# Second expert stage of a two-block decoder kernel: experts 2 to 15 in an order made on chip, and pairs of 96 and 64 slots in place of 96 and 96

## The chip, the cores and the metric

The kernel runs on one core of a Trainium2 chip. Its time is the device time of one launch in microseconds (us). All data are 32-bit floats.

## What is computed

Two decoder blocks run one after the other over 512 tokens of width 1024. Each has a token mixer (not touched here) and a mixture of experts. The second block's mixture has 16 experts in 4 groups; each token goes to two experts of its best group, so 1024 pairs of a token and an expert are to be computed:

```python
N_EXPERTS_2 = 16;  TOP_K = 2;  EXPERT_HIDDEN = 512;  D_MODEL = 1024
def hier_moe_2(x, w_group, b_group, w_expert, b_expert, w_gate, w_up, w_down):
    t = x.reshape(-1, D)
    pg = jax.nn.softmax((t @ w_group + b_group).astype(jnp.float32), axis=-1)
    ...
    gates = jnp.sum(jax.nn.one_hot(expert_id, N_EXPERTS_2, dtype=jnp.float32) * weights[..., None], axis=1)
    for e in range(N_EXPERTS_2):
        h = jax.nn.silu(t @ w_gate[e]) * (t @ w_up[e])
        y = y + gates[:, e:e + 1] * (h @ w_down[e])
```

For the inputs of this case the reference sends 69, 62, 64, 63, 63, 73, 58, 44, 88, 72, 73, 77, 39, 56, 55 and 68 tokens to experts 0 to 15.

## The kernel before

The first block's expert stage (32 experts, weights of 1 MB a matrix) is the "narrow" one and stays as it is. The second block's is the "wide" one (`z.wide`): 8 bodies of two experts, experts 2i and 2i+1 in body i. Each expert has a gate, an up and a down matrix of 2 MB. There is one buffer for each expert of a pair: `z.expert(0)`, called `ring` in the trace, and `z.expert(1)`, called `arena_moe`. A load for the next body can therefore only be issued when TensorE has used the matrix that lies there.

Each expert has 96 slots (`cap`), a body 192: expert A's 96 and expert B's first 32 fill the 128 partitions of units 0 and 1, and expert B's other 64 are unit 2. TensorE works in tiles of 32 rows of output: four such tiles, each with its own 32 tokens and its own part of a weight matrix, run side by side. In a body it makes

- unit 0 of gate and up (`gate_up`, L2385): 8 steps of four products of 512 columns;
- unit 1 and unit 2 (`gates_before_ups`, L2396): each first 8 steps of gates, then 8 of ups, of four products of 256 columns. Unit 2 has the 64 slots of expert B twice, once for each half of the hidden width;
- the turning of the hidden values (`turn_hidden`, L2440) between these;
- the turning of the token rows of the next body (`turn_rows_pe`, L1953), in two halves; for body 1 a gather by products with a one-hot matrix stands in its place (`gather_pe`, L1937);
- `down_first` (L2453): two products of 8 steps for units 0 and 1, and `down_second` (L2465): 4 steps of four products of 512 columns for unit 2.

TensorE's counts that others wait for are `gates`, `hidden` (units done), `down` (down products done). SyncE's queue issues the weights in a fixed order, each after such a count: gate and up of expert A, gate and up of expert B (L1577), down of A, down of B (L1583). GpSimd fetches the token rows of body i+2 from `normed_rows` by an indirect transfer (`fetch_rows`, L1911) and places the results in `expert_rows` (`place_rows`, L1918 and L1921). ScalarE makes the silu and moves the results out of the banks, VectorE multiplies gate by up (L2511) and scales the turned rows (`turned_rows_dve`, L1962).

Which token sits in which slot comes from a table in memory, `slot_table`, with a row for every rank and expert. VectorE counts (`out_programs.rounds`), computes ranks, positions and weights (`entries`), GpSimd writes the table (L1848), SyncE reads it back (`load_slots`, L1591). If an expert has more than 96 tokens, further rounds over all bodies are run from `Further.run`; the largest count decides. In the trace no such round runs.

The last body's rows aren't placed in memory: `all_sums_pe` (L1996) adds them to the residual through products with a one-hot matrix, while eight loads of 512 KB (`load_outputs`, L2039) bring back what the other bodies placed. They are issued when unit 1 of the last body is done. VectorE adds them (`add_outputs_dve`, L2048), makes the low parts of the last body's results (`y_low_dve`, L2025), and adds the sums (`add_sums_dve`, L2055).

Of the kernel before, what the change touches and what calls it, by code (L numbers as in the profile page):

```python
# [15 lines left out]
P = 128  # L16
S = 512
# [1468 lines left out]
class Moe:  # L1486


    def __init__(self, m, d, experts, per_group, slots, block):
# [7 lines left out]
        self.loads = 64 if self.wide else 32  # L1497
        self.most = -(-S // slots)
# [14 lines left out]
        at = self.extra.end  # L1513
        self.now_fetch, at = m.view(at, 2, dt=I32)
# [24 lines left out]
        for i in range(9):  # L1539
            self.one[i], s = m.view(s, NT)  # L1540
        self.ring23, end = m.view(m.arena_size - 2 * RING, 2, RING)
# [24 lines left out]

    def weights_of(self, io, name, e):

        w = io[name][0]
        return w[e] if isinstance(e, int) else w[bass.ds(e, 1)].rearrange("e a b -> (e a) b")  # L1570

    def load_in(self, sp, io, s, body, sem, parts=(0, 1)):

        both, _ = self.expert(s) if self.wide else self.slot(s)
        for k in parts:
            w = self.weights_of(io, self.weights[k], body * self.EB + s)
            sp.dma_start(both[:, k], w.rearrange("(p c) n -> p c n", p=P)).then_inc(sem, 16)  # L1577

    def load_down(self, sp, io, s, body, sem):

        _, down = self.expert(s) if self.wide else self.slot(s)
        w = self.weights_of(io, self.weights[2], body * self.EB + s)
        sp.dma_start(down, w.rearrange("(c p) n -> p c n", p=P)).then_inc(sem, 16)  # L1583

    def load_slots(self, engine, slots, first_rank, sem):
# [7 lines left out]
        if self.wide:  # L1593
            part(0, 0, 0, 0, self.cap)
# [3 lines left out]
        else:  # L1598
            part(0, 0, 0, 0, 64)
            part(64, 0, 1, 0, 64)  # L1600

# [10 lines left out]
def out_programs(m, io, z, ph, residual, residual_scale, w_out_sem, gain, router, ring_sems):  # L1612
# [116 lines left out]
    def vector(dve):  # L1729
# [35 lines left out]
        v.mark(dve.tensor_scalar(z.upper, m.tokens[:, 0:1], float(64 - S), None, ALU.is_ge))  # L1765
        for k in range(2):
# [44 lines left out]
    def entries(dve):  # L1811

        split(dve, NT - 1)
        v = Chain(dve, ph.sem("weights"))
        for k in range(2):
# [15 lines left out]
    def rounds(dve):  # L1831

        v = Chain(dve, ph.sem("counting"))
        dve.wait_ge(ph.sem("totals"), 1)
        v.link(dve.tensor_reduce(z.stat[:, 0, 0:1], m.banks[7][:, 0:E], AX_X, ALU.max))
# [22 lines left out]

def front_products(pe, m, k, chunks):
# [6 lines left out]
class Further:  # L1866
# [5 lines left out]
    def run(self, engine, begin, body, end):  # L1872
# [4 lines left out]
        with engine.If(n > 0):  # L1877
            with engine.Fori(0, n) as r:
                begin(r)
                with engine.Fori(0, z.bodies) as i:  # L1880
                    body(r * z.bodies + i, i)
# [8 lines left out]
def slots_known(engine, z, slots, known, done):  # L1890
# [10 lines left out]
    if z.wide:  # L1901
# [3 lines left out]
    engine.wait_ge(known, done + KNOWN)  # L1905


def fetch_rows(pool, ph, z, fetch):

    for c, count in enumerate((P, z.slots - P)):  # L1910
# [4 lines left out]
def place_rows(pool, ph, z, place, c):  # L1915

    if z.wide and c == 1:
# [8 lines left out]
def gather_pe(pe, ph, z, pair, half, taken, last_split=None):  # L1926

    for a in range(2):
        if taken is not None:
            pe.wait_ge(ph.sem("gathered_taken"), taken + a + 1)  # L1930
        for b in range(2):
            j = 4 * half + 2 * a + b
            for t in range(NT):
                if last_split is not None and j == 0 and t == NT - 1:
                    pe.wait_ge(last_split, NT)
                for part in (z.x_hi, z.x_lo):
                    last = pe.matmul(pair[a][:, b * z.slots:(b + 1) * z.slots], part[:, t, j * P:(j + 1) * P], z.G[:, t, :],  # L1937
# [4 lines left out]
def turn_rows_pe(pe, ph, m, z, pair, half, arrived, taken):  # L1942
# [3 lines left out]
    for a in range(2):  # L1946
        if taken is not None:
            pe.wait_ge(ph.sem("gathered_taken"), taken + a + 1)
        for b in range(2):
            j = 4 * half + 2 * a + b  # L1950
            for c, count in enumerate((P, z.slots - P)):
                at = b * z.slots + c * P
# [4 lines left out]
def turned_rows_dve(dve, ph, m, z, pair, gain, n, half):  # L1957

    for a in range(2):
        dve.wait_ge(ph.sem("gathered"), 4 * n + 2 * half + a + 1)  # L1960
        j = 4 * half + 2 * a
        dve.tensor_tensor(z.xe[:, j:j + 2, :], pair[a][:, 0:2 * z.slots].rearrange("p (j n) -> p j n", j=2),  # L1962
                          m.params[:, gain + j:gain + j + 2].unsqueeze(2).broadcast_to([P, 2, z.slots]),
# [6 lines left out]
def onehot_dve(dve, ph, m, z, body):  # L1970

    cap, e = z.cap, body * z.EB
    if z.wide:
        own = cap - 64
        qa, qb, count = z.q[:, :, e:e + 1], z.q[:, :, e + 1:e + 2], m.slots[:, 1:2, :]
        dve.tensor_tensor(z.G[:, :, 0:cap], count[:, :, 0:cap].broadcast_to([P, NT, cap]), qa.broadcast_to([P, NT, cap]), ALU.is_equal)
        dve.tensor_tensor(z.G[:, :, cap:P], count[:, :, 64:cap].broadcast_to([P, NT, own]),
                          qb.broadcast_to([P, NT, own]), ALU.is_equal).then_inc(ph.sem("onehot"), 1)
        dve.tensor_tensor(z.G[:, :, P:P + 64], count[:, :, 0:64].broadcast_to([P, NT, 64]),
                          qb.broadcast_to([P, NT, 64]), ALU.is_equal).then_inc(ph.sem("onehot"), 1)  # L1980
# [6 lines left out]

def sums_pe(pe, ph, m, z, t, c, last_part):
# [1553 lines left out]
```

## Time and profile before

| what | value |
|---|---|
| median of 3 runs | 1460.3 us (1455.28 to 1463.12) |
| span of the profiled execution | 1458.0 us |
| granted TensorE clock, mean | 0.972 |
| PE busy | 1346.8 us, 92% |
| DVE / ACT / POOL busy | 500.6 / 369.4 / 313.7 us |
| moved by the DMA engines | 284.08 MB, mean 195 GB/s |

The profiled execution's own time is one of those in the first line; what lies around its span isn't given apart, so the span stands 2.3 us under the median. A busy share is a mean over stages with different limits; the second expert stage with its router is the part from about 1130 us on, its eight bodies lie between 1147 and 1439 us.

### The profile page before, as it was taken

The page shows a single profiled execution, that of the slowest core. Times are in us where ns is not written, and L with a number is a line of the kernel's source. Part 1 is how long each engine was busy: PE and PEld are TensorE (multiplying, and loading weights), DVE is VectorE, ACT ScalarE, POOL GpSimd, SP SyncE. Part 2 cuts the span into 40 slices and gives each one's busy share as a digit, 9 for nine tenths or more (in the row PEclk, how much of TensorE's full clock was granted, in tenths as well). Part 3 has the DMA queues.
Part 4 walks back from the last instruction along what each step waited for, and adds up shares of the span by engine and source line. Part 5 has one row for each costly group of instructions (what it writes and reads, how often), then busy time and mean ns, then how long its engine had stood idle before and what let it go on. Part 6 is the DMA issues. An engine that isn't in the chain of part 4 may idle for free. (4 is left out here: it accounts for less than half of the span.)

```text
span 1458.0 us, 27226 instructions
## 1 busy us (share of the span) xinstructions
PE 1346.8 (92%) x11948; PEld 869.5 (60%) x11948; DVE 500.6 (34%) x906; ACT 369.4 (25%) x682; POOL 313.7 (22%) x357
## 2 busy tenths in 40 slices
PE   6999989888899999998969999998899899999995
PEld 4878764577745554454448878895545654444442
DVE  4367425442233321111283167654523201000016
ACT  2223026444133011111142241324423011111112
POOL 8436202255000200000023523440000301111100
PEclk9999999999999999999979999999999899999998
DMA  5911100300062799999941121103062589999983
GB/s 160 342 68 58 58 1 0 117 4 5 4 249 101 280 416 417 415 418 417 411 170 59 58 79 37 59 2 116 1 248 103 209 325 376 387 378 387 381 330 148
DMA packets 75596, 284.08 MB, mean 195 GB/s; under 512 B 15217, under 2 KB 16568, under 8 KB 63186
## 3 DMA queue, kind: packets, MB, share of 16 engines
q1 hardware_dynamic: 68464, 267.47, 47.4%
q0 software_dynamic: 5440, 10.58, 2.1%
q10 hardware_dynamic: 1570, 4.24, 0.7%
q8 instruction: 97, 1.59, 0.5%
q14 instruction: 25, 0.20, 0.0%
HBM read 259.41 MB, written 29.84 MB: 198 GB/s over the span
## 5 line engine op out<-in xcount | busy, mean ns | idle before, releaser
L2396 PE MATMUL banks<-arena_moe,mixT 128*32 128x256 f32 x1280 | 113.5, 379 | 0.0
L391 POOL TENSOR_TENSOR arena_mix<-ring 128x512 f32<-128x512 f32 (+1 forms) x56 | 72.8, 1317 | 173.4 <-PE banks L426 128.3
L436 ACT ACTIVATE arena_mix<-banks 128x256 f32<-128x256 f32 x108 | 41.1, 383 | 258.4 <-PE banks L426 258.4
L1921 POOL DMA_INDIRECT expert_rows<-arena_moe x21 | 20.5, 978 | 388.5 <-ACT arena_moe L2220 161.3
L1648 PE MATMUL banks<-ring,mixT 128*128 128x512 f32 x224 | 99.1, 595 | 3.9 <-PEq L50 3.1
L426 PE MATMUL banks<-ring 128*128 128x256 f32 x432 | 100.1, 380 | 2.7 <-DVE arena_mix L447 1.6
L426 PEld LDWEIGHTS banks<-ring 128*128 128x128 f32 x432 | 81.2, 190 | 16.5 <-issue 5.8
L1962 DVE TENSOR_TENSOR mixT<-banks,params 128x512 f32<-128x512 f32 (+1 forms) x64 | 39.9, 625 | 143.3 <-PE banks L1937 85.3
L447 DVE SCALAR_TENSOR_TENSOR arena_mix<-banks,arena_mix 128x256 f32<-128x256 f32 x81 | 33.1, 422 | 160.2 <-ACT arena_mix L436 90.0
L1937 PE MATMUL banks<-G_moe,x_hi_moe 128*128 128x256 f32 (+1 forms) x320 | 81.3, 294 | 2.9 <-issue 2.9
L426 PE MATMUL banks<-ring,arena_mix 128*128 128x256 f32 x336 | 78.7, 389 | 2.8 <-POOL arena_mix L391 1.9
L1937 PE MATMUL banks<-G_moe,x_lo_moe 128*128 128x256 f32 (+1 forms) x320 | 79.6, 288 | 0.0
L426 PE MATMUL banks<-mixT,ring 128*128 128x256 f32 x336 | 76.8, 383 | 1.3 <-DVE mixT L318 1.3
L426 PEld LDWEIGHTS banks<-ring,arena_mix 128*128 128x128 f32 x336 | 64.8, 195 | 15.9 <-issue 7.2
L2396 PEld LDWEIGHTS banks<-arena_moe,mixT 128*32 128x32 f32 x1280 | 60.3, 109 | 22.0 <-issue 1.3
L1648 PEld LDWEIGHTS banks<-ring,mixT 128*128 128x128 f32 x224 | 41.5, 190 | 52.4 <-issue 52.4
L2511 DVE TENSOR_TENSOR mixT<-mixT,banks 128x256 f32<-128x256 f32 x24 | 10.1, 421 | 177.0 <-ACT mixT L2543 177.0
L426 PEld LDWEIGHTS banks<-mixT,ring 128*128 128x128 f32 x336 | 64.1, 192 | 10.9 <-DVE mixT L318 1.5
L1937 PEld LDWEIGHTS banks<-G_moe,x_hi_moe 128*128 128x128 f32 x320 | 63.9, 200 | 6.0 <-issue 6.0
L2120 PE MATMUL banks<-arena_moe,mixT 128*64 128x512 f32 x256 | 59.9, 621 | 7.1 <-DMA arena_moe<-in_exp_w_up 7.1
L1937 PEld LDWEIGHTS banks<-G_moe,x_lo_moe 128*128 128x128 f32 x320 | 64.0, 200 | 0.0
L2453 PE MATMUL banks<-ring,mixT 128*32 128x512 f32 x384 | 56.5, 594 | 1.9 <-issue 1.9
(453 smaller groups left out, 2564.1 us busy)
## 6 DMA issues: line engine op xcount, KB each, us to landing
ring<-in_w_in SPq DMA_DIRECT2D x26, 1024.0 KB, 7.7
arena_moe<-in_exp_w_gate SPq DMA_DIRECT2D x16, 1024.0 KB, 12.4
arena_moe<-in_exp_w_up SPq DMA_DIRECT2D x16, 1024.0 KB, 16.4
arena_moe<-in_exp_w_down SPq DMA_DIRECT2D x16, 1024.0 KB, 16.0
ring<-in_exp_w_gate SPq DMA_DIRECT2D x16, 1024.0 KB, 11.7
ring<-in_exp_w_up SPq DMA_DIRECT2D x16, 1024.0 KB, 14.3
ring<-in_exp_w_down SPq DMA_DIRECT2D x16, 1024.0 KB, 17.7
arena_moe<-in_w_gate SPq DMA_DIRECT2D x8, 2048.0 KB, 11.7
```

The source lines that it names most:

```text
L391: pool.tensor_tensor(out[:, c], a[:, c], b[:, c], op).then_inc(ph.sem("weight_sums"), 1)
L426: last = pe.matmul(self.m.banks[bank][:, 0:256], left, right, start=(k == 0 and j in (1, 2, 7)), stop=(k == 3), skip_group_check=True)
L436: act.activation(self.dest(n, i)[block], self.m.banks[a][:, 0:256], ACT.Copy, scale=self.scale(n)).then_inc(ph.sem(name), 1)
L447: dve.scalar_tensor_tensor(out, self.m.banks[c if j == 2 else d][:, 0:256], self.scale(n), out, ALU.mult, ALU.add).then_inc(ph.sem(name), 1)
L1648: last = pe.matmul(m.banks[k % 3][:], m.mixT[:, c, i * P:(i + 1) * P], w[:, c, :], start=(c == 0), stop=(c == DC - 1), skip_group_check=True)
L1921: pool.indirect_dma_start(z.d.outputs, bass.IndirectOffsetOnAxis(ap=place[:, c:c + 1].bitcast(U32), axis=0), z.y[:, 2 * c:2 * c + 2, :].re ...
L1937: last = pe.matmul(pair[a][:, b * z.slots:(b + 1) * z.slots], part[:, t, j * P:(j + 1) * P], z.G[:, t, :], start=(t == 0 and part is z.x_h ...
L1962: dve.tensor_tensor(z.xe[:, j:j + 2, :], pair[a][:, 0:2 * z.slots].rearrange("p (j n) -> p j n", j=2), m.params[:, gain + j:gain + j + 2]. ...
L2120: last = pe.matmul(hb[u][k * cap:(k + 1) * cap, :], z.xe[:, j, s * cap:(s + 1) * cap], both[:, :, j, :], start=(j == 0), stop=(j == DC - 1))
L2396: last = pe.matmul(hb[u][T * k:T * (k + 1), 256 * part:256 * part + 256], z.xe[:, j, at:at + T], both[:, part, j, half * 256:half * 256 + ...
L2453: last = pe.matmul(yb[n][T * i:T * (i + 1), :], z.hT[:, h, f, T * i:T * (i + 1)], wd[:, 2 * half + f, n * HW:(n + 1) * HW], start=(h == 0 ...
L2511: dve.tensor_tensor(z.hid[:, u, :], z.hid[:, u, :], hb[u][:, 256:512], ALU.mult).then_inc(ph.sem("hidden_done"), 1)
```

## The change

Bodies 1 to 7 no longer hold experts 2i and 2i+1. VectorE ranks experts 2 to 15 by their counts on chip; the seven with the most tokens take the even positions 2, 4, ..., 14, the other seven the odd ones 3, 5, ..., 15, in order. So body 1 has the largest and the eighth, body 7 the seventh and the last. Body 0 keeps experts 0 and 1 and 96 and 96 slots. A pair of bodies 1 to 7 has 96 and 64 slots: 160. A further round now also runs if more than 7 of experts 2 to 15 have over 64 tokens.

The packing into tiles of 32 is new. Unit 0 (`packed_gate_up`) needs only expert A, unit 1 (`packed_gates_before_ups`) has the rest of A and two tiles of B, and the third unit (`packed_rest`) is B's last 32 slots: its four tiles are gate and up, each in two halves, of 256 columns, half a unit. `packed_down_second` has products of 256 columns. Its results are quarters of a row, which `place_rows` writes as quarters, and which `quarter_sums_pe` sums in the last body.

```diff
@@ order_experts, new; called at the start of entries()
+    v.link(dve.scalar_tensor_tensor(z.keys, z.totals, float(E), z.tie, ALU.mult, ALU.add))
+    v.link(dve.tensor_tensor(z.pairs[:, 2:, 1:], z.keys[:, 1:].unsqueeze(1).broadcast_to([P, E - 2, E - 1]),
+                             z.keys[:, 2:].unsqueeze(2).broadcast_to([P, E - 2, E - 1]), ALU.is_gt))
+    v.link(dve.tensor_reduce(z.greater[:, 2:], z.pairs[:, 2:, 1:], AX_X, ALU.add))
...
+    return dve.tensor_copy(z.expert_at, z.greater)
@@ sync of wide_programs
-        z.load_slots(sp, z.main, 0, ph.sem("slots"))
+        load_main_slots(sp, z, ph.sem("slots"))
+        sp.wait_ge(out.sem("ordered"), 1)
         for i in range(1, NB):
-            for s in range(2):
-                sp.wait_ge(ph.sem("gates"), 2 * i + s - 1)
-                z.load_in(sp, io, s, i, ring[s], (0,))
-                sp.wait_ge(ph.sem("hidden"), 3 * i + s - 1)
-                z.load_in(sp, io, s, i, ring[s], (1,))
+            e = [chosen(2 * i + s) for s in range(2)]
+            sp.wait_ge(ph.sem("gates"), 1 if i == 1 else i + 1)
+            z.load_in(sp, io, 0, i, ring[0], (0,), e[0])
+            sp.wait_ge(ph.sem("hidden"), 3 * i - 1)
+            z.load_in(sp, io, 0, i, ring[0], (1,), e[0])
+            if i == 1:
+                sp.wait_ge(ph.sem("gates"), 2)
+            else:
+                sp.wait_ge(ph.sem("hidden"), 3 * i)
+            z.load_in(sp, io, 1, i, ring[1], (0,), e[1])
+            sp.wait_ge(ph.sem("hidden"), 3 * i)
+            z.load_in(sp, io, 1, i, ring[1], (1,), e[1])
@@ tensor of wide_programs, the third unit and the second down product of bodies 1 to 7
+        def packed_rest(i):
+
+            both, _ = z.expert(1)
+            for j in range(DC):
+                for k in range(4):
+                    part, half = k // 2, k % 2
+                    last = pe.matmul(hb[2][T * k:T * (k + 1), 0:256], z.xe[:, j, P:P + T],
+                                     both[:, part, j, half * 256:half * 256 + 256], start=(j == 0), stop=(j == DC - 1),
+                                     skip_group_check=True)
+            last.then_inc(ph.sem("hidden"), 1)
...
+            for h in range(2):
+                for f in range(2):
+                    for k in range(4):
+                        last = pe.matmul(yb[2][T * k:T * (k + 1), 0:256], z.hT[:, 2, f, T * h:T * h + T],
+                                         wd[:, 2 * h + f, 256 * k:256 * k + 256], start=(h == 0 and f == 0),
+                                         stop=(h == 1 and f == 1), skip_group_check=True)
@@ quarter_sums_pe, new
+    for flip in range(2):
+        if flip == 1:
+            pe.wait_ge(ph.sem("quartered"), 2 * t + 4)
+        for part in (z.y_hi, z.y_lo):
+            for k in range(2):
+                g = (k + flip) % 2
+                for n in range(2):
+                    a = 64 * n + 32 * g
+                    last = pe.matmul(m.banks[2 * (t + k) + n][:, 256 * g:256 * g + 256], z.ST[a:a + 32, 1, (t + k) * P:(t + k + 1) * P],
+                                     part[a:a + 32, 2, 0:256], start=False, stop=(part is z.y_lo), skip_group_check=True)
```

Where the instructions stand. On TensorE, in the last body, the pieces around the third unit and the second down product. Before:

```order
L2396 MATMUL banks<-ring,mixT 32x256 x3
L2396 MATMUL banks<-arena_moe,mixT 32x256
L2440 MATMUL banks<-ident,mixT 128x128 x2
L2396 MATMUL banks<-arena_moe,mixT 32x256 x64
L2440 MATMUL banks<-ident,mixT 128x128 x2
L2453 MATMUL banks<-ring,mixT 32x512 x3
L2453 MATMUL banks<-arena_moe,mixT 32x512
L2440 MATMUL banks<-ident,mixT 128x128 x2
L2465 MATMUL banks<-arena_moe,mixT 32x512 x16
L1996 MATMUL banks<-x_hi_moe,G_moe 128x512 x32
```

After:

```order
L2580 MATMUL banks<-ring,mixT 32x256 x2
L2580 MATMUL banks<-arena_moe,mixT 32x256 x2
L2670 MATMUL banks<-ident,mixT 128x128 x2
L2591 MATMUL banks<-arena_moe,mixT 32x256 x32
L2670 MATMUL banks<-ident,mixT 128x128 x2
L2614 MATMUL banks<-ring,mixT 32x512 x3
L2614 MATMUL banks<-arena_moe,mixT 32x512
L2600 MATMUL banks<-ident,mixT 128x64 x2
L2626 MATMUL banks<-arena_moe,mixT 32x256 x16
L2135 MATMUL banks<-x_hi_moe,G_moe 128x512 x8
L2122 MATMUL banks<-x_hi_moe,G_moe 128x256 x16
L2135 MATMUL banks<-x_hi_moe,G_moe 128x512 x8
```

The third unit has 32 products for 64, the second down product 16 of 256 columns for 16 of 512; nothing moved past anything else, and the trace counts each of these products as two records.

On VectorE, between the one-hot matrix of body 0 and the ranks. Before:

```order
L1979 TENSOR_TENSOR G_moe<-slots,arena_moe 128x4x64
L1727 TENSOR_TENSOR x_lo_moe<-arena_moe,x_hi_moe 128x1024
L1816 TENSOR_TENSOR arena_moe<-arena_moe 128x64 x2
L1819 TENSOR_REDUCE arena_moe<-arena_moe 128x4 x2
L1821 TENSOR_REDUCE arena_moe<-arena_moe 128x4
```

After:

```order
L1764 TENSOR_TENSOR x_lo_moe<-arena_moe,x_hi_moe 128x1024
L1940 SCALAR_TENSOR_TENSOR arena_moe<-arena_moe 128x16
L1941 TENSOR_TENSOR arena_moe<-arena_moe 128x14x15
L1943 TENSOR_REDUCE arena_moe<-arena_moe 128x14
L1944 TENSOR_SCALAR arena_moe<-arena_moe 128x14
L1945 SCALAR_TENSOR_TENSOR arena_moe<-arena_moe 128x14
L1946 TENSOR_SCALAR arena_moe<-arena_moe 128x16
L1948 TENSOR_TENSOR arena_moe<-arena_moe,experts 128x256
L1949 TENSOR_TENSOR arena_moe<-arena_moe,experts 128x256
L1950 TENSOR_REDUCE arena_moe<-arena_moe 128x16
L1951 CAST arena_moe<-arena_moe 128x16
L1857 TENSOR_TENSOR arena_moe<-arena_moe 128x64 x2
```

Ten operations of the ordering stand ahead of the ranks, ten more for ranks by position follow them, and the counting of rounds before this piece has nine operations for four.

On SyncE's queue, between the down loads of one body and the gate load of the next. After (before, L1583 for expert B is followed by L1577 at once):

```order
L1601 DMA ring<-in_w_down 128x4x1024
L1601 DMA arena_moe<-in_w_down 128x4x1024
L2486 TENSOR_LOAD arena_moe
L2486 ISA x2
L2486 TENSOR_LOAD arena_moe
L2486 ISA x2
L1595 ISA
L1595 DMA ring<-in_w_gate 128x4096
L1595 DMA ring<-in_w_up 128x4096
```

Two reads of an expert's number into registers stand ahead of each body's loads (an ISA row is a wait or a register step).

## Rows read from the trace of the kernel before

**Rows 1.** The page, part 2: 40 slices of 36.45 us, GB/s moved.

```profile
GB/s 160 342 68 58 58 1 0 117 4 5 4 249 101 280 416 417 415 418 417 411 170 59 58 79 37 59 2 116 1 248 103 209 325 376 387 378 387 381 330 148
```

**Rows 2.** Chain that ended last, 1170 to 1439 us: start, duration, what.

```profile
1170.48 3.56 PE banks L1937 x32
...
1188.54 6.87 PE banks L2385 x64
...
1260.34 6.87 PE banks L2385 x64
...
1274.49 7.04 PE banks L2396 x128
...
1283.60 7.01 PE banks L2453 x64
...
1292.67 3.57 PE banks L2465 x32
1296.24 6.87 PE banks L2385 x64
...
1425.50 1.88 issue
1427.38 7.07 PE banks L2453 x64
...
1438.93 2.73 PE banks L1996 x12
```

**Rows 3.** Timeline of SyncE's queue: start, duration, line, transfer issued.

```profile
1198.92 0.34 SPq L1577 DMA_DIRECT2D ring<-in_w_gate  x1
...
1260.45 0.38 SPq L1583 DMA_DIRECT2D arena_moe<-in_w_down  x1
1270.72 0.34 SPq L1577 DMA_DIRECT2D ring<-in_w_gate  x1
...
1417.77 0.34 SPq L2039 DMA_DIRECT2D ring<-expert_rows  x1
```

**Rows 4.** Windows 1200 to 1202 us: engines, granted clock, DMA share, GB/s.

```profile
1200.00:1201.00 1.00, 1.00 (x24) 0.65 (x20) 0.00 (x0) 0.00 (x0) 0.00 (x0) 1.00 0.46 98
1201.00:1202.00 1.00, 1.00 (x27) 0.54 (x16) 0.00 (x0) 0.00 (x0) 0.00 (x0) 1.00 1.05 426
```

**Rows 5.** DMA view of one body, 1260.34 to 1296.24 us.

```profile
DMA packets 2038, 13.66 MB, mean 381 GB/s; under 512 B 248, under 2 KB 248, under 8 KB 1523
...
q1 hardware_dynamic: 1587, 12.40, 88.5%
q0 software_dynamic: 448, 1.21, 10.8%
...
arena_moe<-in_w_down SPq DMA_DIRECT2D x1, 2048.0 KB, 13.8
```

**Rows 6.** DMA view, 500 to 700 us, the first expert stage.

```profile
DMA packets 15960, 83.38 MB, mean 417 GB/s; under 512 B 2336, under 2 KB 2336, under 8 KB 9254
```

**Rows 7.** Windows of 2 us within the same body.

```profile
1266.34:1268.34 2.00, 2.00 (x37) 0.97 (x31) 0.42 (x1) 0.38 (x1) 0.00 (x0) 1.00 1.03 293
...
1284.34:1286.34 2.00, 2.00 (x24) 0.65 (x20) 0.00 (x0) 0.00 (x0) 0.00 (x0) 1.00 1.04 442
```

**Rows 8.** VectorE's timeline, 1129 to 1150 us.

```profile
1129.25 0.23 DVE L1792 TENSOR_TENSOR arena_moe<-arena_moe 128x64 f32<-128x64 f32 x1
...
1141.31 0.56 DVE L1962 TENSOR_TENSOR mixT<-banks,params 128x384 f32<-128x384 f32 x1 [4.04 <-PE banks L1937]
...
1149.62 1.02 DVE L1962 TENSOR_TENSOR mixT<-banks,params 128x384 f32<-128x384 f32 x2 [5.17 <-remote]
```

**Rows 9.** Timeline, 1433 to 1442 us, the end of the stage.

```profile
1433.07 1.23 DVE L2048 TENSOR_TENSOR arena_moe<-arena_moe 128x1024 f32<-128x1024 f32 x1
...
1434.21 0.75 DVE L2025 SCALAR_TENSOR_TENSOR x_hi_moe<-banks,arena_moe,x_hi_moe 128x512 fp32r<-128x512 f32 x1
...
1441.78 2.35 DVE L2055 TENSOR_TENSOR arena_moe<-arena_moe,banks 128x1024 f32<-128x1024 f32 x2 [1.31 <-PE banks L1996]
```

More of the change, by code:

```diff
@@ L1540, in __init__ @@
             self.one[i], s = m.view(s, NT)
+        if self.wide:
+            self.totals, s = m.view(s, experts)
+            self.keys, s = m.view(s, experts)
+            self.pairs, s = m.view(s, experts, experts)
+            self.greater, s = m.view(s, experts)
+            self.later, s = m.view(s, experts)
         self.ring23, end = m.view(m.arena_size - 2 * RING, 2, RING)
@@ L1593, in load_slots @@
         if self.wide:
-            part(0, 0, 0, 0, self.cap)
+            part(0, 0, 0, 32, self.cap)
             part(self.cap, 0, 1, 64, self.cap - 64)
@@ L1814, in entries @@
         v = Chain(dve, ph.sem("weights"))
+        if z.wide:
+            order_experts(dve, v, m, z).then_inc(ph.sem("ordered"), 1)
+            for k in range(2):
+                v.mark(dve.tensor_tensor(t[4 + k], t[k], z.later.unsqueeze(1).broadcast_to([P, NT, E]), ALU.mult))
+            v.wait()
+            for k in range(2):
+                v.mark(dve.tensor_reduce(one[7 + k], t[4 + k], AX_X, ALU.add))
+            second_ranks(dve, v, z, t[4], t[5])
         for k in range(2):
@@ L1870, in __init__, with run @@
         self.m, self.z, self.known = m, z, known
-    def run(self, engine, begin, body, end):
+    def run(self, engine, begin, body, end, written_out=False):
         z = self.z
@@ L1879, in run @@
                 begin(r)
-                with engine.Fori(0, z.bodies) as i:
-                    body(r * z.bodies + i, i)
+                if written_out:
+                    for i in range(z.bodies):
+                        body(r * z.bodies + i, i)
+                else:
+                    with engine.Fori(0, z.bodies) as i:
+                        body(r * z.bodies + i, i)
             end(n)
@@ L2399, in gates_before_ups, with packed_gate_up @@
                 last.then_inc(ph.sem("gates" if part == 0 else "hidden"), 1)
+        def packed_gate_up(i):
+            pe.wait_ge(ring[0], 32 * i + 32)
+            for j in range(DC):
+                if j % 2 == 0:
+                    pe.wait_ge(ph.sem("gathered_taken"), 4 * i + j // 2 + 1)
+                for k, (s, at, half) in enumerate(packed[0]):
+                    both, _ = z.expert(s)
+                    last = pe.matmul(hb[0][T * k:T * (k + 1), :], z.xe[:, j, at:at + T], both[:, :, j, half * 256:half * 256 + 256],
+                                     start=(j == 0), stop=(j == DC - 1), skip_group_check=True)
+            last.then_inc(ph.sem("hidden"), 1)
@@ new lines, in packed_gates_before_ups @@
+        def packed_gates_before_ups(i):
+            pe.wait_ge(ring[1], 32 * i + 32)
+            for part in range(2):
+                for j in range(DC):
+                    for k, (s, at, half) in enumerate(packed[1]):
+                        both, _ = z.expert(s)
+                        last = pe.matmul(hb[1][T * k:T * (k + 1), 256 * part:256 * part + 256], z.xe[:, j, at:at + T],
+                                         both[:, part, j, half * 256:half * 256 + 256], start=(j == 0), stop=(j == DC - 1),
+                                         skip_group_check=True)
+                last.then_inc(ph.sem("gates" if part == 0 else "hidden"), 1)
@@ new lines, in packed_rest @@
+        def packed_rest(i):
+            both, _ = z.expert(1)
+            for j in range(DC):
+                for k in range(4):
+                    part, half = k // 2, k % 2
+                    last = pe.matmul(hb[2][T * k:T * (k + 1), 0:256], z.xe[:, j, P:P + T],
+                                     both[:, part, j, half * 256:half * 256 + 256], start=(j == 0), stop=(j == DC - 1),
+                                     skip_group_check=True)
+            last.then_inc(ph.sem("hidden"), 1)
```

302 lines of the change are left out of this document (228 added, 74 removed).

## Prediction

> **What bounds the kernel now.** The change lies in the second expert stage, the last 310 us. I read the page's slices first: there the transfers run at 376 to 387 GB/s through the stage, against 415 to 418 in the first expert stage [rows 1]. So both the weights' transfers and TensorE could be the limit, and the next view must say which. The chain of work that ended last is TensorE alone: each body repeats the same pieces, body 3 begins at 1260.34 and body 4 at 1296.24, 35.90 us apart, with no wait in between [rows 2]; the other bodies repeat this to 0.1 us. TensorE is the limit.
>
> The reader must then ask how far behind the transfers are. SyncE issues expert B's down load at 1260.45; it lands 13.8 us later, at 1274.3, while the next body's first gate load was issued at 1270.72 [rows 3, 5]. The queue has not emptied when the next load enters. In that one body the 16 DMA engines moved 13.66 MB and were taken 88.5% by the weights' queue and 10.8% by the token rows' queue [rows 5]: 99.3% of 35.9 us. The transfers are a second limit just under the first.
>
> **The change, part by part.**
>
> TensorE. A packed body (1 to 7) has a third gate-and-up unit of half the columns, and a second down product of half the columns. The unit of 256-column products takes 7.04 us, the down product 3.57 [rows 2]; half of each is 3.52 and 1.79. That a 256-column product costs half of a 512-column one can be seen in the same rows: 64 of 512 columns take 6.87 us, 128 of 256 take 7.04. The transposes of the rows keep their number; I give them nothing. So a body falls from 35.90 to 30.6 us. For seven bodies (the last too) TensorE alone would save 37 us. The token rows of body 1 are gathered in 160 columns for 192: from nothing to 1.2 us (a sixth of its two pieces of 3.56 [rows 2]); I take nothing.
>
> Transfers. Nothing is taken away from them. The same sixteen experts are loaded, in another order, and only real tokens' rows are fetched and placed, about 128 a body as before. So a body still needs the 13.66 MB. What time does it need for them when TensorE no longer sets the pace? From below: the first expert stage sustained 417 GB/s over 200 us [rows 6], which gives 32.8 us. From above: the 35.9 us that it has now, of which the engines are taken 99.3%. Inside a body the rate is 442 GB/s while gates and ups are loaded, and 293 while down loads and token rows run side by side [rows 7]. The own mix is the nearer row, which speaks for the upper end. But in a queue that is never short of work the token rows will fall beside other loads, and the gaps between loads close, as in the first stage. I choose 34.2 us, near the middle. This is above 30.6: **the transfers become the limit.**
>
> The chain of the transfers. Body 1 starts at 1188.54 and its first 10.3 us are as before, so gate load 2 is issued at 1198.92 [rows 3] and the queue, which had been idling, fills at 1201.0 [rows 4]. From there it always has work: in a packed body the two down loads enter at 26.8 and 30.6 us, the next gate load 10.3 later. Each body adds 34.2 us. The down weights of body 7 are there at 1201.0 + 6 x 34.2, less 2 us since the last of these bodies fetches no rows (half of its token traffic, 10.8% of 35.9) = 1404.2. TensorE alone would be at body 7's first down product at 1188.54 + 6 x 30.6 + 18.0 (14.15 for two units and a turn, 3.52, 0.37 for a turn) + 1.9 (the stall before it, the 1.88 marked issue) = 1392.0. The later one counts: 1404.2 in place of 1427.38 [rows 2], a gain of 23.2 us. Bodies 1 and 2 run at 30.6; the first wait for down weights is in body 3 or 4.
>
> The end. After the last down weights SyncE's queue holds eight loads of placed rows, 4.19 MB, now issued at 1417.77 [rows 3], in time. They will stand behind the down loads: at 381 GB/s 11.0 us, until 1415.2. VectorE then adds the last two parts (2 x 1.23) and only behind them makes two low parts (2 x 0.75) [rows 9]: 1419.2, and the final sums begin. TensorE is ready at 1404.2 + 9.7 (11.5 from 1427.38 to 1438.93, less 1.79) = 1413.9. So the sums begin 15.0 us after the down product, and not 11.5: 3.5 us given back. The sums themselves are split in quarters, in two rounds with a wait of TensorE on its own results: not shown by any row; from nothing (four products side by side) to 1.5 us (half the time from 1438.93 to the first add at 1441.78 [rows 2, 9]); I take 0.6.
>
> The front. VectorE gets some 25 more small operations ahead of the entries of the slot table, each step about 0.23 us [rows 8]: 5.9 us. Behind them stand the first multiplication of the gathered rows, which TensorE waits for, and the slot table. VectorE had idled 4.0 us before that multiplication and 5.2 before the third [rows 8], so most is covered: nothing to 5.9 us, I take 1.5. The table comes 6 us later, but its rows are wanted only at the end of body 1. The register loads of the expert numbers stand on SyncE between the last down load and the next gate load, where it waits 10.3 us (1260.45 to 1270.72, [rows 3]): nothing, as long as two of them take less.
>
> Sum: 23.2 - 3.5 - 0.6 - 1.5 = 17.6 us, so 1458.0 becomes 1440.4. The median of the three runs stands 2.3 above the profiled span; with it **1443 us**.
>
> **The rivals.**
>
> A, forecast: the queue of the transfers takes over, at 32.8 to 35.5 us a body. Chance 0.75.
>
> B, the queue has no room: the slow mix of down loads and token rows is a matter of the chip and stays, 35.9 us a body. For it: 99% taken now. Against: 417 GB/s over 200 us [rows 6]. Body 7's down weights come at 1414.4, the gain is 13.0 - 5.6 = 7.4 us: 1453. Chance 0.13. The Trainium skill goes further this way: its page "SBUF — State Buffer", section "Summary: rules for kernel authors", says to reckon with about 358 GB/s between HBM and SBUF, by which a body's 13.66 MB would need 38 us and no cut on TensorE could help. By that rule the trace disagrees (381 GB/s over this body), and the skill's "HBM Reference", section "Specifications (TRN2)", has about 425 for a core that streams alone, which the 417 and 442 bear out.
>
> C, TensorE stays the limit: it needs the queue to do a body in under 31 us, 440 GB/s with the token rows in it; only windows without such rows show that [rows 7]. Gain 35.4 - 2.1: 1427. Chance 0.04.
>
> D, the other side: the loads now take their address from a register, and no load of the stage before did. If the queue can't prepare such a load while another runs, each pays the start again: the queue stood nearly 2.1 us from issue to full rate (1198.92 to 1201.0, [rows 3, 4]). Six a body are 12.6 us, 46.8 us a body; after six of them 75.6 us more than the forecast, 1518 us. It decides from 0.5 us a load (17.6 / 36 loads). Nothing in the rows speaks for it. Chance 0.05. (Were over 7 of experts 2 to 15 above 64 tokens, a whole further round would come; for these inputs 6 are.)
>
> The rest, 0.03, is a front or an end that costs more than a few us.
>
> **The numbers.** With 32.8 us a body the gain is 26.0 (1434), with 35.9 it is 7.4 (1453); the front may cost 4.4 more or 1.5 less. Range 1432 to 1454. Half a per cent (7.3 us) is what a measurement can tell. Slower: D and a little, 0.06. Same: over half of B and of the rest, 0.09. Faster: 0.85.
>
> **What would show it.** The chain of the stage, now TensorE alone, has waits for the down weights in bodies 3 or 4 to 7, some 3.5 us each, and starts of bodies 34.2 us apart where the first ones lie 30.6 apart. GB/s rises to 400 over a body. The third unit shows 64 products in 3.5 us. The final sums wait for VectorE's low parts. It would be wrong if bodies stay 30.6 apart to the end (C), if they lie above 35.5 apart (B or D), or if body 0 starts more than 4 us later.

## The result, and the profile after

| | kernel before | changed kernel |
|---|---|---|
| median, 4 runs each | 1461.7 us (1455.3 to 1467.4) | **1440.7 us** (1439.4 to 1443.1) |
| ratio to before | | 0.987, 95% interval 0.984 to 0.990 |
| span of the profiled execution | 1458.0 us | 1438.9 us |
| PE busy | 1346.8 us, 92% | 1313.6 us, 91% |
| DVE busy | 500.6 us | 506.9 us |
| moved by the DMA engines | 284.08 MB | 284.03 MB |

The change takes 21 us off, 15 to 23 by the interval. 1443 was forecast, 1432 to 1454 as range.

The page's slices of the changed kernel, GB/s moved in each 36 us, beside [rows 1]:

```profile
GB/s 162 344 71 59 59 1 0 118 4 5 4 233 93 275 414 418 415 417 416 415 243 33 86 59 59 59 1 102 17 139 142 206 307 350 409 411 412 394 392 150
```

The slices of the stage, 376 to 387 before, are 409 to 412 now. The chain that ended last, beside [rows 2] (start, duration, what):

```profile
1186.83 6.87 PE banks L2569 x64
1193.70 6.91 PE banks L2580 x128
...
1200.98 3.59 PE banks L2591 x64
...
1215.53 1.86 PE banks L2626 x32
1217.39 6.87 PE banks L2569 x64
1224.26 6.91 PE banks L2580 x127
...
1235.75 20.47 DMA arena_moe<-in_w_up
1256.26 7.11 PE banks L2580 x128
...
1267.96 22.25 DMA arena_moe<-in_w_up
1290.26 8.80 PE banks L2580 x127
...
1303.65 19.65 DMA arena_moe<-in_w_up
1323.34 7.12 PE banks L2580 x128
...
1335.04 24.24 DMA arena_moe<-in_w_up
1359.33 8.81 PE banks L2580 x128
...
1384.93 6.87 PE banks L2569 x64
1391.80 7.16 PE banks L2580 x122
```

Body 1 takes 30.56 us (1186.83 to 1217.39), with the third unit at 3.59 and the second down product at 1.86. Then each of bodies 3 to 6 has one wait in the chain, always at the same place: unit 1 (L2580) waits for expert B's up matrix. That load is issued right behind the third unit of the body before, which frees its buffer, and lands 20 to 24 us later, where a load needs 5 us of the engines alone (2.1 MB at 412 GB/s): it stands behind others in the queue. Unit 1 takes 7.1 us behind some waits and 8.8 behind others: in those the granted clock was at the lower level for a part of the unit (0.50 from 1292 to 1294, where it is 1.00 through the unit at 1323.34).

The chain doesn't show every wait. These four come to 9.1 us (1.44, 3.22, 0.62 and 3.78), and TensorE waits once more, for the down weights of body 5, on a stretch that the chain does not go through:

```profile
1337.73 0.63 PE L2614 MATMUL banks<-ring,mixT 128*32 128x512 f32 x3 [1.36 <-DMA arena_moe<-in_w_down]
```

The DMA view of 100 us in the middle of the stage (1260 to 1360), before and then after:

```profile
DMA packets 5815, 38.17 MB, mean 382 GB/s; under 512 B 808, under 2 KB 808, under 8 KB 4378
```

```profile
DMA packets 6137, 41.22 MB, mean 412 GB/s; under 512 B 708, under 2 KB 708, under 8 KB 4592
```

The share of packets under 512 B is near the same (14% and 12%) and the rate is 8% higher. The timelines of TensorE and VectorE at the end (the bracket is the idle time ahead and who ended it), beside [rows 9]:

```profile
1405.11 0.63 PE L2614 MATMUL banks<-ring,mixT 128*32 128x512 f32 x3 [1.87 <-issue]
...
1412.82 1.93 PE L2626 MATMUL banks<-arena_moe,mixT 128*32 128x256 f32 x32 [0.37 <-ACT mixT L2805]
1417.60 3.55 PE L2135 MATMUL banks<-x_hi_moe,G_moe 128*128 128x512 f32 x8 [2.84 <-DVE x_hi_moe L2170]
1421.08 0.57 PE L2122 MATMUL banks<-x_hi_moe,G_moe 32*128 32x256 f32 x8
1421.80 0.51 PE L2122 MATMUL banks<-x_hi_moe,G_moe 32*128 32x256 f32 x8 [0.15 <-PE banks L2122]
```

```profile
1405.22 1.22 DVE L2193 TENSOR_TENSOR arena_moe<-arena_moe,ring 128x1024 f32<-128x1024 f32 x1 [5.41 <-DMA arena_moe<-expert_rows]
...
1416.04 1.80 DVE L2170 SCALAR_TENSOR_TENSOR x_hi_moe<-banks,arena_moe,x_hi_moe 128x512 fp32r<-128x512 f32 x3
1422.62 2.35 DVE L2200 TENSOR_TENSOR arena_moe<-arena_moe,banks 128x1024 f32<-128x1024 f32 x2 [4.78 <-PEq L2127]
```

TensorE waits 2.84 us for VectorE's low parts, which stand behind eight early additions; the sums then run at the lower clock (0.53 granted; 3.55 us for eight products, where the next eight of that size take 2.08 in the same timeline).

**Where the 19.1 us between the two spans come from.** Part of it lies ahead of the stage, in code that the change doesn't touch: the last group of products of the routing (L1672, now L1709) starts at 1123.46 before and at 1119.94 after, 3.5 us. From there to body 1: 65.08 before, 66.89 after, 1.8 lost. From body 1 to the last body's first down product: 238.84 and 218.28, 20.6 gained. From there to the first of the last additions (L2055, now L2200): 14.40 and 17.51, 3.1 lost. The rest is equal. 3.5 - 1.8 + 20.6 - 3.1 = 19.2.

### The profile page after: what moved, and what is told of

The parts are those of the page before. It is cut to its first block and busy times, and to the rows that moved or that the text cites. A ratio compares the mean times of both kernels' runs of the same rounds, so it can differ in the third digit from the quotient of the medians.

```text
span 1438.9 us, 26499 instructions
## 1 busy us (share of the span) xinstructions
PE 1313.6 (91%) x11516; PEld 854.5 (59%) x11516; DVE 506.9 (35%) x938; ACT 367.1 (26%) x682; POOL 313.6 (22%) x358
## 2 busy tenths in 40 slices
DMA packets 75339, 284.03 MB, mean 197 GB/s; under 512 B 14966, under 2 KB 16317, under 8 KB 62930
## 5 line engine op out<-in xcount | busy, mean ns | idle before, releaser
L2081 DVE TENSOR_TENSOR mixT<-banks,params 128x512 f32<-128x512 f32 (+2 forms) x64 | 38.1, 596 | 139.3 <-PE banks L2056 80.5
L2056 PE MATMUL banks<-G_moe,x_hi_moe 128*128 128x256 f32 (+2 forms) x320 | 82.2, 296 | 2.8 <-issue 2.8
L2056 PE MATMUL banks<-G_moe,x_lo_moe 128*128 128x256 f32 (+2 forms) x320 | 80.5, 291 | 0.0
L426 PEld LDWEIGHTS banks<-ring,arena_mix 128*128 128x128 f32 x336 | 64.1, 192 | 13.3 <-issue 4.9
L2580 PE MATMUL banks<-ring,mixT 128*32 128x256 f32 x448 | 53.0, 398 | 9.1 <-DMA arena_moe<-in_w_up 9.1
L2757 DVE TENSOR_TENSOR mixT<-mixT,banks 128x256 f32<-128x256 f32 x17 | 7.2, 421 | 139.9 <-ACT mixT L2797 139.9
L2265 PE MATMUL banks<-ring,mixT 128*64 128x512 f32 x256 | 56.3, 592 | 0.0
L2321 DVE TENSOR_TENSOR mixT<-mixT,banks 128x256 f32<-128x256 f32 x16 | 6.7, 422 | 131.9 <-ACT mixT L2355 131.9
## 6 DMA issues: line engine op xcount, KB each, us to landing
ring<-in_exp_w_gate SPq DMA_DIRECT2D x16, 1024.0 KB, 12.8
ring<-in_exp_w_down SPq DMA_DIRECT2D x16, 1024.0 KB, 17.6
```

Source lines behind the costliest of these rows:

```text
L426: last = pe.matmul(self.m.banks[bank][:, 0:256], left, right, start=(k == 0 and j in (1, 2, 7)), stop=(k == 3), skip_group_check=True)
L2056: last = pe.matmul(pair[a][:, b * width:(b + 1) * width], part[:, t, j * P:(j + 1) * P], z.G[:, t, 0:width], start=(t == 0 and part is z.x ...
L2081: dve.tensor_tensor(z.xe[:, j:j + 2, 0:width], pair[a][:, 0:2 * width].rearrange("p (j n) -> p j n", j=2), m.params[:, gain + j:gain + j + ...
L2265: last = pe.matmul(hb[u][k * cap:(k + 1) * cap, :], z.xe[:, j, s * cap:(s + 1) * cap], both[:, :, j, :], start=(j == 0), stop=(j == DC - 1))
L2580: last = pe.matmul(hb[1][T * k:T * (k + 1), 256 * part:256 * part + 256], z.xe[:, j, at:at + T], both[:, part, j, half * 256:half * 256 + ...
```

## The experiments

Since what lies ahead of the stage moves from profile to profile, the runs are read within it. The columns, worked out from the chain or timeline of each profiled execution: start of the last group of routing products; from there to body 1; from unit 1 of body 1 to unit 1 of body 7 (six bodies); from there to the first of the last additions. Then the time: the median of four to eight executions, of two for the changed kernel with half down, and of a single one for three quarters, fewer rows, fixed addresses, longer front and both fillings of the wait.

| run | routing | to body 1 | six bodies | end | time, us |
|---|---|---|---|---|---|
| kernel before | 1123.5 | 65.1 | 215.4 | 31.0 | 1461.7 |
| changed kernel | 1119.9 | 66.9 | 198.1 | 30.8 | 1440.7 |
| before, half down | 1123.1 | 64.4 | 215.4 | 31.0 | 1462.0 |
| after, half down | 1122.6 | 65.8 | 183.4 | 30.0 | 1428.7 |
| after, three quarters | 1130.2 | 64.0 | 185.6 | 30.1 | 1434.7 |
| after, fewer rows | 1124.0 | 63.0 | 195.5 | 29.4 | 1437.4 |
| after, fixed addresses | 1119.3 | 66.5 | 197.4 | 30.2 | 1438.3 |
| before, longer front | 1124.0 | 66.8 | 215.4 | 31.0 | 1462.0 |
| after, four products in the wait | 1126.0 | 62.5 | 198.5 | 28.6 | 1440.3 |
| after, two products in the wait | 1125.8 | 67.4 | 198.6 | 28.5 | 1445.0 |
| after, two rows to a partition | 1122.7 | 67.0 | 197.8 | 29.7 | 1443.2 |
| after, low parts first | 1128.2 | 63.8 | 198.3 | 28.1 | 1438.3 |
| after, finer order | 1118.4 | 66.6 | 198.0 | 28.6 | 1442.6 |
| after, both edits | 1131.0 | 66.8 | 197.4 | 27.3 | 1442.8 |

### Is it the transfers? Half of the down weights, in both kernels

```diff
@@ load_down
-        sp.dma_start(down, w.rearrange("(c p) n -> p c n", p=P)).then_inc(sem, 16)
+        kept = 2 if self.wide and body > 0 else down.shape[1]
+        sp.dma_start(down[:, 0:kept], w.rearrange("(c p) n -> p c n", p=P)[:, 0:kept]).then_inc(sem, 16)
```

> The changed kernel with only half of each down matrix loaded for bodies 1 to 7 (the results of those experts are wrong for that half; every product is still made). Theory, the transfers limit the changed stage: a body needs 11.6 MB for 13.7, about 28 us of the queue, less than TensorE's 30.6. The waits for weights in bodies 3 to 6 go, all bodies start 30.6 us apart, body 7's first down product comes 203 us after body 1's start and not 218, and the final sums no longer wait for VectorE's low parts: 1440.7 becomes about 1423. Rival, the bodies' 33 to 35 us come from something else than the amount moved (addresses from registers, the slower clock, the order in which buffers come free): under 4 us faster, bodies still 33 us and more apart.

> The kernel before with the same halving of its down loads (wrong results for that half). Theory, TensorE alone limits the stage before: bodies stay 35.9 us apart and the span stays within 2 us of 1458. Rival, the transfers were already sharing the limit: bodies under 35.5 us apart, at least 3 us faster.

The kernel before doesn't notice: ratio 1.002 (1.000 to 1.004), bodies 35.90 us apart to the last digit. The changed one falls to 1428.7 us, ratio 0.978 (0.974 to 0.982), and bodies are 30.57 apart with no wait. The windows view of six bodies (busy us of each engine, granted clock, DMA share, GB/s), with half down and in the changed kernel:

```profile
1186.83:1385.00 198.17, 198.17 (x2448) 90.07 (x2444) 20.88 (x45) 24.41 (x56) 22.88 (x23) 1.00 0.90 355
```

```profile
1186.83:1385.00 198.17, 187.75 (x2249) 84.80 (x2244) 20.46 (x44) 23.55 (x55) 21.90 (x22) 0.98 0.99 398
```

TensorE is busy throughout in the one and stands still for 10.4 us in the other, where the DMA engines are taken 99%. That share alone would prove nothing, since before it was as high [rows 5] and TensorE set the pace; the two runs do. So TensorE alone limited before, and the transfers limit now. The time is 5.7 us above the 1423 expected: the sums still wait 2.15 us for VectorE's low parts and run at the lower clock, of which more below, and the profiled execution reached the stage 2.7 us later than the changed kernel's.

The dose between, three quarters of each down matrix (`kept = 3`):

> The changed kernel, but bodies 1 to 7 load only three quarters of each down matrix: 12.6 MB a body in place of 13.6, results computed with stale values in the last quarter. Theory (a body needs the time of its packets, 33.3 us with both down matrices, 10.8 of them for down weights): three quarters need 33.3 - 2.7 = 30.6 us, just TensorE's 30.57, so bodies lie 30.6 to 31 us apart, waits at unit 1 are under 0.5 us each, and the time is 1428 to 1431 us. Rival (something else than bytes, such as the register addresses or the order of the queue, keeps 33 us a body): above 32.5 us a body, over 1436.

Six bodies take 185.6 us, 30.9 each, as expected, with one wait left, of 2.0 us where under 0.5 was expected. The time is 3.7 us above the upper end of what was expected; this execution reached the stage 10.3 us later than the changed kernel's (1130.2 for 1119.9).

### The register addresses

```diff
-            e = [chosen(2 * i + s) for s in range(2)]
+            e = [(8, 3, 11, 4, 5, 6, 10, 13, 9, 14, 15, 7, 2, 12)[2 * i - 2 + s] for s in range(2)]
```

> The changed kernel with the 14 expert numbers of these inputs written as constants in SyncE's loads; VectorE still makes the order. Theory, an address from a register costs nothing: the same gate-load issue times after TensorE's counts within 0.3 us, the same mean distance of bodies 2 to 6 (33 to 34 us), span within 3 us of 1439. Rival D of the prediction, each load pays for the register: bodies at least 1 us closer together, down to 30.6, span 5 us and more shorter.

Six bodies take 197.4 us for 198.1, with much the same waits (8.6 us for up loads and 1.3 for a down load, for 9.1 and 1.4). Rival D falls: by this one pair of profiles the addresses from registers cost about 0.1 us a body.

### The front

```diff
@@ entries, kernel before, ahead of the ranks
+        if z.wide:
+            for k in range(24):
+                v.link(dve.tensor_tensor(t[4], t[0], t[1], ALU.add))
```

> The kernel before with 24 more small chained VectorE operations (6 us) where the change puts its ordering, results unused. Theory, most of it is covered by VectorE's idle time: body 1 starts 0 to 3 us later, counted from the end of the projection on TensorE, near the 1.8 us by which the changed kernel is late there. Rival, it is on the path in full: 5 to 6 us later.

The way to body 1 is 66.8 us in place of 65.1 and 64.4: about 2 us. But the later runs show that this way isn't fixed to better than that: with the changed kernel's own front it is 62.5 to 67.4 us. In the four shortest (62.5 to 64.0) the first unit of body 0 runs through; in all the others, the kernel before among them, TensorE stops one to three times in it, and each time the next product starts 0.2 to 1.7 us late. From the chains of the run with four products in the wait and of the changed kernel:

```profile
1148.75 7.01 PE banks L2545 x64
```

```profile
1144.99 4.49 PE banks L2545 x36
...
1149.88 1.30 PE banks L2545 x5
1151.31 2.38 PE banks L2545 x20
```

The profile names no releaser for these stops, and whether a longer front brings any of them about was not settled. What the ordering costs is lost in this spread: it isn't shown to be more than nothing, nor more than 2 us.

### Does the slower clock behind a wait cost time?

```diff
@@ packed_body
+            if 3 <= i <= 6:
+                for _ in range(4):
+                    pe.matmul(hb[1][:], m.after[:], z.h[:, 0, 0:HW], start=True, stop=True)
             packed_gates_before_ups(i)
```

> The changed kernel with four more products of 512 columns on TensorE ahead of unit 1 in bodies 3 to 6, where TensorE waits for expert B's up load. Their results go to a bank that is overwritten; nothing is left out. They take about 1.7 us and hold TensorE at work during the wait. Theory (transfers set the distance of bodies, and the slower clock behind a wait costs nothing because the next wait takes it up): unit 1 takes 7.0 to 7.2 us in all bodies, in place of 8.8 in two of them, and the distance from unit 1 of body 1 to unit 1 of body 7 stays 198.1 +- 1.5 us. Rival (the slower clock is part of what sets the distance): 194 to 195 us.

I had the price of these products wrong: they take 3.63 us, not 1.7, which brings TensorE's own work to 34.3 us a body and fills the wait whole. Six bodies took 198.5 us, but now TensorE could have set that itself (4 x 34.3 and 2 x 30.6), so the run told nothing apart. Hence the next, with two (`range(2)`):

> As the run with four products put into the wait of bodies 3 to 6, but with two. There each took 0.9 us, 3.7 for the four, and TensorE itself came to 34.34 us a body in these four bodies; that filled the wait whole, so the run couldn't tell the two theories apart. Two take 1.7 to 1.9 us and leave 0.5 to 1.5 us of wait. Theory (transfers set the distance, the slower clock behind a wait costs nothing): 198.1 +- 1.5 us from unit 1 of body 1 to unit 1 of body 7, waits for the up load are still there. Rival (the slower clock costs 3.4 to 3.8 us of it): 194 to 195 us.

Its chain:

```profile
1230.65 6.91 PE banks L2580 x122
1261.21 1.91 PE banks L2720 x4
1263.13 7.05 PE banks L2580 x124
1274.77 21.79 DMA arena_moe<-in_w_up
1296.60 7.12 PE banks L2580 x128
1308.30 22.68 DMA arena_moe<-in_w_up
1331.03 7.12 PE banks L2580 x122
1342.74 23.20 DMA arena_moe<-in_w_up
1365.98 7.11 PE banks L2580 x128
1377.69 20.89 DMA arena_moe<-in_w_up
1398.63 6.45 PE banks L2580 x113
```

Unit 1 now takes 6.9 to 7.2 us everywhere, and the distance is still 198.6 us. Body 3's wait is filled whole, and body 7, which had none, waits 1.87 us. So 3.4 us of slower clock less and 7.6 us of added products more change nothing: both are paid out of TensorE's waits. The transfers set the distance to the very last body.

### What sets the transfers' rate: packets or bytes?

```diff
@@ load_down
+        if self.wide:
+            sp.dma_start(down.rearrange("p (h f) n -> p h f n", h=2), w.rearrange("(h p f) n -> p h f n", h=2, f=2)).then_inc(sem, 16)
@@ turn_hidden, turn_rest
-                last = pe.transpose(hb[u][:, f * P:(f + 1) * P], z.hid[:, u, f * P:(f + 1) * P], m.ident[:])
+                last = pe.transpose(hb[u][:, f * P:(f + 1) * P], z.hid[:, u, f:256:2], m.ident[:])
```

> The changed kernel with another layout of the down matrices of the second stage: a partition holds rows 2p and 2p+1 of each half in place of p and 128+p, so that a packet is 8 KB of memory in place of 4 KB; the turning of the hidden values takes every second column to match. Nothing is left out. In the changed kernel 4.19 MB of down weights take 10.8 us of the engines (388 GB/s) and 8.39 MB of gate and up 19.7 us (426 GB/s) in 16 KB packets. Theory (transfers set the distance, and small packets are the slow part of the mix): 0.5 to 0.95 us less for each of six bodies, unit 1 of body 1 to unit 1 of body 7 is 192.5 to 195 us in place of 198.1, the time 3 to 6 us less, 1435 to 1438 beside 1440.7. Rival (down weights are slower because token rows run beside them, not for the size of their packets): 197.5 to 198.5 us.

The DMA view of the same 100 us as above:

```profile
DMA packets 4571, 41.16 MB, mean 412 GB/s; under 512 B 721, under 2 KB 721, under 8 KB 1462
```

The packets under 8 KB fell from 4592 to 1462, and the rate is 412 GB/s as in the changed kernel. Six bodies take 197.8 us, the time is 1443.2 us (ratio 0.988, 0.986 to 0.990), as the rival had it. My theory that 4 KB packets are the slow part is wrong.

Taking token rows away instead:

```diff
@@ fetch_rows
-    for c, count in enumerate((P, width - P)):
+    for c, count in enumerate((P, width - P) if width != 160 else (32, 32)):
```

> The changed kernel, but for bodies 2 to 7 GpSimd fetches token rows only for 32 of the 128 partitions of the first part (the second part of 32 as before); the other rows stay those of an earlier body, so the results of these bodies are not the reference's. The rows of a body take 2.8 us of the engines, about half of it for fetching; three quarters of that falls away where slots are filled, 0.9 to 1.1 us a body. Theory (transfers set the distance, rows included): unit 1 of body 1 to unit 1 of body 7 takes 192 to 194 us in place of 198.1, and about 4 to 5 us less in all. Rival (the row transfers fit into gaps of the loads and cost nothing): 197 to 198 us.

Six bodies take 195.5 us, 2.6 less: more than the rival's, less than the theory's. The row transfers aren't free, but they cost about their bytes. Over 100 us GpSimd's queue moved 2.37 MB in place of 2.96; at 412 GB/s that is 1.4 us, or 2.8 over six bodies. The theory had counted 96 rows a body as gone; by the moved bytes it was about 50 (0.2 MB).

### The end

```diff
@@ vector, last body
         early(2)
-        early(3)
         for i in range(3):
             y_low_dve(dve, ph, z, i, yb[i], ...)
+        early(3)
```

> The changed kernel with one piece moved on VectorE: in the last body the three low parts of its results are made behind the second of the five pairs of early additions, not behind the fifth. Nothing is left out. Theory (the end waits for the low parts because they stand behind additions that wait for the loads of the placed rows, which stand behind the last down loads): the final sums then begin right behind the second down product, near 1415 us in place of 1417.6; as TensorE hasn't idled, its clock stays up and the first eight products take about 1.8 us in place of 3.55; the first of the last additions starts near 1418.2 in place of 1422.6, so the kernel takes 3.5 to 4.5 us less than the changed one, 1436 to 1437.5 beside its 1440.7. Rival (the placed rows themselves are late: the early additions that are left then end too late and the last additions wait for VectorE instead): less than 1 us gained.

In the finer order, the three low parts and the two additions of `early(3)` stand as low, addition, low, low, addition:

> The changed kernel with VectorE's end in a finer order: three pairs of early additions, first low part, an addition, second and third low part, the last early addition. Nothing is left out. With three low parts ahead of the fourth pair, VectorE idled 1.45 and 1.20 us between low parts and then held the first of the last additions by 2.4 us of early ones. Theory: the idle time takes one of them, the first of the last additions comes 13.3 to 14.3 us behind the first down product of the last body where TensorE's clock is full (14.8 there with a slow down product, 17.6 in the changed kernel), and the kernel takes 3 to 5 us less than the changed one, 1436 to 1437.7. Rival (data of the fourth pair or TensorE's sums end last, so that the order no longer matters): as with the low parts ahead of the fourth pair, within 0.5 us.

> The two edits together, the down matrices with two rows to a partition and VectorE's end in the finer order. Nothing is left out. If transfers set the distance of the bodies and the end hangs on VectorE's order, they add up: 6 to 10 us less than the changed kernel, 1431 to 1435. If packets of 4 KB aren't the cause, it stands where the finer order alone stands, 1436 to 1438.

With the finer order, VectorE and TensorE at the end:

```profile
1412.23 0.75 DVE L2170 SCALAR_TENSOR_TENSOR x_hi_moe<-banks,arena_moe,x_hi_moe 128x512 fp32r<-128x512 f32 x1
1412.90 1.21 DVE L2193 TENSOR_TENSOR arena_moe<-arena_moe,ring 128x1024 f32<-128x1024 f32 x1
1414.03 0.74 DVE L2170 SCALAR_TENSOR_TENSOR x_hi_moe<-banks,arena_moe,x_hi_moe 128x512 fp32r<-128x512 f32 x1
```

```profile
1414.92 2.08 PE L2135 MATMUL banks<-x_hi_moe,G_moe 128*128 128x512 f32 x8 [0.47 <-DVE x_hi_moe L2170]
```

TensorE's wait shrinks from 2.84 to 0.47 us and the sums keep the upper clock. The first of the last additions comes 13.6 us behind the first down product (1404.81 to 1418.42) in place of 17.5, as expected. With the low parts first it is 14.8, where 13.1 was expected: there the first down product ran at the lower clock for a while (0.50 granted from 1411 to 1413) and took 8.77 us for 7.07. Not all of this is the order's doing. In the two runs with the old order where the sums ran at the upper clock, both with products in the wait, the addition comes 15.2 and 15.5 us behind; so the order itself is worth 1 to 2 us (13.6 here, 14.1 with both edits), and the rest is the clock. In the last column of the table it is 27.3 to 28.6 us with either order, against 29.4 to 30.8 in most runs with the old one, but 28.5 and 28.6 in the two where the clock happened to stay up. (The 28.6 of the finer order has a unit 1 of 8.8 us in it, behind a wait.) The timing doesn't confirm a gain: 1438.3, 1442.6 and 1442.8 us, where 1436 to 1437.5, 1436 to 1437.7 and 1431 to 1438 were expected; ratios 0.984 (0.981 to 0.988), 0.988 (0.986 to 0.990) and, for both edits, 0.986 (0.984 to 0.988), against 0.987 of the changed kernel. Some 2 us are there in the profiles, part of them the clock's; what lies ahead of the stage varies by 13 us between the profiles (1118.4 to 1131.0) and hides them. No version here is shown to beat the changed kernel.

## Why the prediction was right, point by point

- **What limits.** Right, and shown from both sides by the two runs with half the down weights: TensorE alone before, the transfers after. Rival B (no room, 35.9 us a body) falls, since the rate rose to 412 GB/s as soon as TensorE asked for it, near the 417 of [rows 6]. Rival C falls with the waits, rival D with the fixed addresses. On the rule that I weighed there: the Trainium skill's page "SBUF — State Buffer", section "Summary: rules for kernel authors", reckons with about 358 GB/s, and the trace disagrees (412 over 100 us).
- **TensorE's body, 30.6.** 30.56; third unit 3.59 for 3.52, second down product 1.86 for 1.79.
- **34.2 us a body of transfers.** 33.5 (1224.26 to 1391.80, five bodies). The last down load was forecast 215.7 us behind the start of body 1; it was issued at 1384.99 and took 17.7 us by the DMA view, so landed 215.9 behind. That agrees more closely than the method deserves: the queue was a little faster than forecast and had been filled a little later.
- **The wait for down weights.** This step failed. Forecast were waits for them of some 3.5 us in each body from 3 or 4 to 7. The waits are at unit 1, for expert B's up load, 9.1 us in four bodies, and only body 5 waits for down weights, 1.36 us. The two down loads behind the up load need 10.2 us (4.2 MB at 412 GB/s) and some rows; TensorE needs 12.8 from unit 1 to the down product (1193.70 to 1206.52), and 13.3 in the last body with the 1.87 us stall. So once TensorE has waited at unit 1, little is left to wait for at the down product; both numbers were at hand. In bodies 3 to 7 expert B's down weights landed 12.8, 12.4, 14.3, 11.7 and 10.9 us behind the start of unit 1. Why they took longest in body 5 was not worked out. For the forecast it costs 2.4 us in the last body: the down product started at 1405.11, the weights were there at 1402.7. The gain up to there was 20.6 us, where 23.2 was forecast.
- **The end, 3.5 + 0.6.** The sums do wait for the low parts, but not for the reason given. I had the output loads queue behind the down loads. From their issue to the first low part it is 1398.97 to 1416.04, 17.1 us; it was 16.4 before (1417.77 to 1434.21 [rows 3, 9]) and 16.4 with half the down weights (1385.62 to 1401.99), where no queue stands ahead. So the queue is 0.7 us of it; the rest is that eight additions of 1.23 us and the loads' own time stayed as long as they were while TensorE's pieces above them became 5.3 us shorter (half a unit and half a down product). The wait moved the sums by 1.0 us (12.5 behind the down product for 11.5), not 3.5. The quarter sums cost 0.6 at the upper clock (3.5 us from the sums' start to the first addition in five of the runs, for 2.92), as forecast; the fall of the clock behind the wait, not forecast, added 1.5. Together 3.1 for 4.1.
- **The front, 1.5.** 1.8 in the profiled pair, but this can't be told from the spread of that stretch (62.5 to 67.4 us).
- **The sum.** 20.6 - 3.1 - 1.8 = 15.7 us by the stage, where 17.6 was forecast; the median moved by 21. The difference lies ahead of the stage, where the changed kernel's profile is 3.5 us early. Since other profiles of kernels with the same code there are up to 7.5 us late, I take it for spread and no effect of the change. The table bears this out: on average the routing comes at 1124.4 us in the eleven profiles of the changed kernel and its variants, and at 1123.5 in the three of the kernel before and its own. So the stage's gain came out about 2 us short of the forecast, and that the median came within 3 us of 1443, on its better side, is luck.

## What to carry to other kernels

When two limits lie close, the gain of relieving one is what the other leaves. The average rate while the first still limited (382 GB/s) isn't the second's capacity: look for a stretch where the queue is never short of work. To place the wait that will appear, compare for each awaited load what stands behind it in the queue with what the engine does between its use and the next one's; the load with the least work ahead of its use binds first. This finds the main wait, not every one: a down load was waited for too, once. And work that was hidden under an engine that became faster, here VectorE's eight additions, is the next wait even if nothing about it changed.

## What was not expected of the hardware

- The rate of a full queue was the same with the down matrices in packets of 4 KB and of 8 KB: 412 GB/s with 4592 or 1462 packets under 8 KB in 100 us.
- Behind a wait of TensorE the clock sometimes fell and sometimes not. At the end, sums behind 2.84, 2.44, 2.44, 2.15, 1.91 and 1.91 us of idling took 3.55, 3.45, 3.02, 3.65, 2.67 and 2.96 us for eight products (granted clock 0.51 to 0.74), but behind 2.31 and 2.01 they took 2.08 (1.00). Behind 0.47 and 0.87 it stayed up. The length of the idle time alone doesn't decide.
- Six bodies of the kernel before took 215.40 us in each of three profiles, but the code ahead of them differed by 13 us between profiles of kernels that are equal there.
